# First phase of an encoder block: sine tables two steps later, gated weights in three parts, a third value buffer, and 20 instead of 25 weight conversions

## The reference

```python
h = rms_norm(x, norm1_gain)
proj = h @ w_in                      # (B, S, 1984)
g_q, g_k, g_v, g_gate, g_lr_f, g_lr_b, m_q_a, m_kv_a, m_k_rope = split(proj)
# A: gated linear attention, both directions, from g_q, g_k (256 columns each),
#    g_v (512), g_gate (512), g_lr (2 x 16)
# B: latent attention: mq = rms_norm(m_q_a) @ w_qb, mkv = rms_norm(m_kv_a) @ w_kvb,
#    norms per head, rotation of 32 of 96 columns by cos/sin(position * inv_freq), softmax
x = x + concat([gla_out, mla_out]) @ w_out
h = rms_norm(x, norm2_gain)
x = x + hierarchical_moe(h)          # 32 experts in 4 groups, top 1 group, top 2 experts
```

## Time and profile before

| What | Value |
|---|---|
| Median of 3 runs | 1159.68 us |
| Profiled execution | 1163.62 us |
| Span of core 7, first to last instruction | 1161.9 us |
| Spans of cores 0 to 3 | 1132.9, 1146.5, 1147.5, 1131.8 us |
| Spans of cores 4 to 7 | 1129.2, 1158.3, 1149.3, 1161.9 us |
| First reciprocal of cores 0 to 3 | 261.2, 279.0, 282.9, 261.2 us |
| First reciprocal of cores 4 to 7 | 259.7, 283.0, 266.3, 280.0 us |
| Busy over the span, core 7 | TensorE 69%, ScalarE 54%, VectorE 45%, GpSimd 41% |

### The profile page before, as it was taken

How to read it: one execution, slowest core, us unless ns; L and a number is a source line. 1 busy time by engine, 2 the same in 40 slices (tenths; PEclk the granted TensorE clock), 3 DMA queues, 4 the chain that set the end, 5 groups by cost and what they waited for, 6 DMA issues and landing times.

```text
span 1161.9 us, 18961 instructions; the slowest of 8 cores (1129.2 to 1161.9 us)
## 1 busy us (share of the span) xinstructions
PE 806.2 (69%) x5171; PEld 412.1 (35%) x5171; DVE 523.6 (45%) x857; ACT 627.4 (54%) x1008; POOL 471.3 (41%) x571
## 2 busy tenths in 40 slices
PE   0478778966787787888885786867612877655464
PEld 0244344432222222323221343433202765444452
DVE  3376547622666566666653335463650221221121
ACT  3568577736999999777773233333311543432231
POOL 3054446641555656434410211414243565444333
PEclk9789889988999999999998688777855998888887
DMA  8926976794878777888873587446786699999984
GB/s 145 176 90 116 128 166 127 124 154 99 122 119 132 113 116 101 127 106 118 134 153 81 101 166 197 94 143 152 203 212 216 166 243 244 246 257 262 264 204 75
DMA packets 87949, 179.86 MB, mean 155 GB/s; under 512 B 19129, under 2 KB 37339, under 8 KB 87780
## 3 DMA queue, kind: packets, MB, share of 16 engines
q0 software_dynamic: 36960, 82.53, 48.8%
q1 hardware_dynamic: 50580, 96.04, 27.7%
q10 hardware_dynamic: 304, 0.07, 0.0%
HBM read 201.75 MB, written 93.45 MB: 254 GB/s over the span
## 4 chain that ended last, share of the span: by engine, by line
PE 34%; ACT 15%; SPq 15%; issue 12%; DVE 12%; DMA 10%; POOL 1%; DVEq 1%; ACTq 1%; POOLq 0%
PE pb L444 32%; SPq L417 14%; ACT pbuf L421 7%; DVE rcb L1015 3%; DMA wsl<-w_bf 2%; PE pb L448 2%; DMA v_sp<-vst 2%; ACT sqj L421 2%; DMA xt<-x 2%; DVE PV L429 1%; DMA qk_sp<-qkst 1%; ACT L421 1%; DVE smb L429 1%; ACT sqn L421 1%; ACT rso L421 1%
## 5 line engine op out<-in xcount | busy, mean ns | idle before, releaser
L421 ACT ACTIVATE pbuf<-pb 128x1024 bf16<-128x1024 f32 x256 | 254.2, 1021 | 46.6 <-PE pb L444 43.9
L444 PE MATMUL pb<-pbuf,vA 128*128 128x512 bf16 x512 | 156.8, 382 | 55.3 <-ACT pbuf L421 53.3
L444 PE MATMUL pb<-qhT,khT 96*128 96x512 bf16 x512 | 155.0, 383 | 4.5 <-issue 4.5
L1015 DVE RECIPROCAL rcb<-pb 64x512 f32<-64x512 f32 x32 | 107.4, 3355 | 89.1 <-PE pb L444 88.9
L444 PE MATMUL pb<-xT,wsl 128*128 128x192 bf16 x1024 | 98.9, 262 | 45.8 <-DMA wsl<-w_bf 43.9
L444 PEld LDWEIGHTS pb<-xT,wsl 128*128 128x128 bf16 x1024 | 92.7, 104 | 49.8 <-issue 48.0
L1141 POOL DMA_INDIRECT out<-zb,LTm x32 | 50.9, 1592 | 117.7 <-ACT xT L421 53.1
L429 DVE TENSOR_TENSOR hid<-sil,pb 128x384 bf16<-128x384 f32 x32 | 17.7, 554 | 176.7 <-PE pb L444 166.0
L548 POOL DMA_DIRECT2D w_bf<-w_exp x112 | 58.5, 528 | 81.8 <-DVE mixM L429 39.1
L444 PEld LDWEIGHTS pb<-pbuf,vA 128*128 128x128 bf16 x512 | 35.4, 96 | 152.3 <-issue 144.8
L429 POOL TENSOR_TENSOR rg<-rg,gqkr 128x512 f32<-128x512 f32 (+1 forms) x32 | 32.1, 1002 | 120.0 <-DVE rg L429 117.7
(11 more groups left out here) (170 smaller groups left out, 1521.7 us busy)
## 6 DMA issues: line engine op xcount, KB each, us to landing
w_bf<-w_exp POOLq DMA_DIRECT2D x112, 384.0 KB, 7.3
wsl<-w_bf SPq DMA_DIRECT2D x112, 384.0 KB
xt<-x SPq DMA_DIRECT2D x32, 512.0 KB
out<-PV SPq DMA_DIRECT2D x16, 512.0 KB
wsl<-w_exp POOLq DMA_DIRECT2D x16, 384.0 KB
qk_sp<-qkst SPq DMA_DIRECT2D x16, 256.0 KB
PV<-qk_sp SPq DMA_DIRECT2D x16, 256.0 KB
h_tok<-hb SPq DMA_DIRECT2D x16, 256.0 KB
```

The source lines that it names most:

```text
L421: return op("act", lambda e: e.activation(out=out, in_=in_, func=func, **kw), reads=reads, writes=writes, n=fsz(out))
L444: return op("pe", lambda e: e.matmul(out, lhsT=lhsT, rhs=rhs, start=start, stop=stop), reads=reads, writes=writes, n=fsz(rhs) * (4 if rhs. ...
L1015: op("dve", lambda e, vrows=vrows, srows=srows, ob=ob: e.reciprocal(out=rcb[vrows, :], in_=P[ob][srows, :]), reads=[PN[ob]], writes=["rcb" ...
```

## The change

It touches the first phase and the table that spreads the conversions.

1. `rope_tables` becomes a generator. Its VectorE part stays where it was, with two tiles `yy0` and `yy1` in place of `yy`; its four ScalarE instructions move to the end of step 1.
2. `w_in_gla` is loaded as three loads of 512 columns with a name each (`wgqk`, `wgv`, `wgg`), the two `wlr` loads before the third, and 32 unused columns are not loaded. Each block waits only for its own part.
3. `vst` has a third tile.
4. `B2Q` interleaves the kinds: k, v, k / q, v, q / v, lr, v / four g.
5. `stage_small` runs in steps 4 to 6 rather than 5 to 7. Pieces: two in each of steps 7 to 16 (20 in all) rather than two or three in each of steps 8 to 17 (25). The attention rounds take three in six rounds of seven, 80 in all rather than 75.

```diff
--- before.py
+++ after.py
@@ -497,7 +497,7 @@
         wm = R("w_in_mla", [128, 8, 416], BF16)
         wqb = R("wqb", [128, 2, 768], BF16)
         wkvb = R("wkvb", [128, 1024], BF16)
-        wg = R("w_in_gla", [128, 8, 1568], BF16)
+        wg = R("w_in_gla", [128, 8, 1536], BF16)
         wlr = R("wlr", [128, 8, 64], BF16)
         cs = R("cs", [128, NT, 64], F32)
         gqa = R("gqa", [128, 384], F32)
@@ -521,7 +521,7 @@
         qkf = [R("qkf%d" % i, [128, 16, 96], BF16) for i in range(3)]
         MR = region(M0, QH0)
         qkst = [MR("qkst%d" % i, [128, 512], F32) for i in range(3)]
-        vst = [MR("vst%d" % i, [128, 512], BF16) for i in range(2)]
+        vst = [MR("vst%d" % i, [128, 512], BF16) for i in range(2)] + [R("vst2", [128, 512], BF16)]
         sgst = [MR("sgst%d" % i, [128, 512], BF16) for i in range(4)]
         lrst = MR("lrst", [64, 512], F32)
         waug = MR("waug", [64, 512], F32)
@@ -530,7 +530,7 @@
         kk = TR("kk", [128, NT, 16], F32)
         ki = TR("ki", [128, NT, 16], I32)
         rr = TR("rr", [128, NT, 16], F32)
-        yy = TR("yy", [128, NT, 16], F32)
+        yyL = [TR("yy%d" % i, [128, NT, 16], F32) for i in range(2)]
         m_ = TR("m_", [128, NT, 16], F32)
 
         ORDER = [g_ * 8 + j for j in range(8) for g_ in range(4)]
@@ -563,9 +563,11 @@
         dma("pool", wm[:, :, :], win_d.ap()[:, 1568:1984].rearrange("(c p) n -> p c n", p=128), writes=["wm"])
         dma("pool", wqb[:, :, :], wqb_d.ap().rearrange("(c p) n -> p c n", p=128), writes=["wqb"])
         dma("pool", wkvb[:, :], wkvb_d[:, :], writes=["wkvb"])
-        dma("pool", wg[:, :, :], win_d.ap()[:, 0:1568].rearrange("(c p) n -> p c n", p=128), writes=["wg"])
+        for nm_, c0_, c1_ in (("wgqk", 0, 512), ("wgv", 512, 1024)):
+            dma("pool", wg[:, :, c0_:c1_], win_d.ap()[:, c0_:c1_].rearrange("(c p) n -> p c n", p=128), writes=[nm_])
         dma("pool", wlr[:, :, 0:16], win_d.ap()[:, 1536:1552].rearrange("(c p) n -> p c n", p=128), reads=["wlr"], writes=["wlra"])
         dma("pool", wlr[:, :, 32:48], win_d.ap()[:, 1552:1568].rearrange("(c p) n -> p c n", p=128), reads=["wlr"], writes=["wlrb"])
+        dma("pool", wg[:, :, 1024:1536], win_d.ap()[:, 1024:1536].rearrange("(c p) n -> p c n", p=128), writes=["wgg"])
         dma("sp", gqa[:, 0:256], bcast_row(gqa_d, 256), writes=["gqaq"])
         dma("sp", gqa[:, 256:384], bcast_row(gkva_d, 128), writes=["gqak"])
         dma("sp", gqk[:, 0, :], bass.AP(gqn_d, 64, [[0, 128], [1, 32]]), writes=["gqkq"])
@@ -605,19 +607,19 @@
             stt(rr[:, :, :], kk[:, :, :], -C1, ang[:, :, :], ALU.mult, ALU.add, ["kk", "ang"], ["rr"])
             stt(rr[:, :, :], kk[:, :, :], -C2, rr[:, :, :], ALU.mult, ALU.add, ["kk", "rr"], ["rr"])
             for which, shift in ((1, 0.0), (0, PI / 2)):
...
-                if which == 0:
-                    act(cs[:, :, 0:16], yy[:, :, :], AF.Sin, ["yy"], ["cs"])
-                    act(cs[:, :, 16:32], yy[:, :, :], AF.Sin, ["yy"], ["cs"])
-                else:
-                    act(cs[:, :, 48:64], yy[:, :, :], AF.Sin, ["yy"], ["cs"])
-                    act(cs[:, :, 32:48], cs[:, :, 48:64], AF.Copy, ["cs"], ["cs"], scale=-1.0)
-            S.alias(["khT"], ["ang", "kk", "ki", "rr", "yy", "m_"])
+                yy, yn = yyL[which], "yy%d" % which
...
+            yield
+            act(cs[:, :, 0:16], yyL[0][:, :, :], AF.Sin, ["yy0"], ["cs"])
+            act(cs[:, :, 16:32], yyL[0][:, :, :], AF.Sin, ["yy0"], ["cs"])
+            act(cs[:, :, 48:64], yyL[1][:, :, :], AF.Sin, ["yy1"], ["cs"])
+            act(cs[:, :, 32:48], cs[:, :, 48:64], AF.Copy, ["cs"], ["cs"], scale=-1.0)
+            S.alias(["khT"], ["ang", "kk", "ki", "rr", "yy0", "yy1", "m_"])
 
         SQ2 = math.sqrt(2.0)
 
@@ -742,10 +744,10 @@
             if kind == "v":
                 t = 4 * g + idx
                 for kc in range(8):
-                    mm(P[bk][:, :], hT[:, kc, hslot(t)], wg[:, kc, 512:1024], kc == 0, kc == 7, [hname(t), "wg"], [PN[bk]])
-                st_ = vst[t % 2]
-                cp("dve", st_[:, :], P[bk][:, :], [PN[bk]], ["vst%d" % (t % 2)])
-                dma("sp", vsp[t * 128:(t + 1) * 128, :], st_[:, :], reads=["vst%d" % (t % 2)], writes=["vsp%d" % t])
+                    mm(P[bk][:, :], hT[:, kc, hslot(t)], wg[:, kc, 512:1024], kc == 0, kc == 7, [hname(t), "wgv"], [PN[bk]])
+                st_ = vst[t % 3]
+                cp("dve", st_[:, :], P[bk][:, :], [PN[bk]], ["vst%d" % (t % 3)])
+                dma("sp", vsp[t * 128:(t + 1) * 128, :], st_[:, :], reads=["vst%d" % (t % 3)], writes=["vsp%d" % t])
                 S.dma_since_barrier.pop()
                 return
             for kc in range(8):
@@ -758,7 +760,7 @@
                 else:
                     lhsT = wlr[:, kc, :]
                 mrows = 64 if kind == "lr" else 128
-                mm(P[bk][0:mrows, :], lhsT, hT[:, kc, gs], kc == 0, kc == 7, hn + ["wg", "wlra", "wlrb"], [PN[bk]])
+                mm(P[bk][0:mrows, :], lhsT, hT[:, kc, gs], kc == 0, kc == 7, hn + {"q": ["wgqk"], "k": ["wgqk"], "g": ["wgg"], "lr": ["wlra", "wlrb"]}[kind], [PN[bk]])
             if kind in ("q", "k"):
                 u = nst["qk"] % 3
                 nst["qk"] += 1
@@ -781,12 +783,13 @@
                 dma("sp", lrsp[g * 64:(g + 1) * 64, :], lrst[:, :], reads=["lrst"], writes=["lrsp%d" % g])
                 S.dma_since_barrier.pop()
 
-        B2Q = [[("k", 0), ("k", 1), ("q", 0)], [("q", 1), ("v", 0), ("v", 1)], [("v", 2), ("v", 3), ("lr", 0)],
+        B2Q = [[("k", 0), ("v", 0), ("k", 1)], [("q", 0), ("v", 1), ("q", 1)], [("v", 2), ("lr", 0), ("v", 3)],
                [("g", 0), ("g", 1), ("g", 2), ("g", 3)]]
         st_A1(0)
         late_consts()
         st_A1(1)
-        rope_tables()
+        rope = rope_tables()
+        next(rope)
         for step in range(NT + 5):
             def has(k):
                 return 0 <= step - k < NT
@@ -819,10 +822,12 @@
                 st_Lr(step - 2)
             while bq:
                 b2_block(*bq.pop(0))
-            if step in (5, 6, 7):
-                stage_small(step - 5)
-            elif 8 <= step <= 17:
-                for _ in range(2 + step % 2):
+            if step == 1:
+                next(rope, 0)
+            if step in (4, 5, 6):
+                stage_small(step - 4)
+            elif 7 <= step <= 16:
+                for _ in range(2):
                     stage_piece()
         S.barrier()
         PVf = A("PV", [128, NT, D], F32, at=W0)
@@ -1015,7 +1020,7 @@
                 op("dve", lambda e, vrows=vrows, srows=srows, ob=ob: e.reciprocal(out=rcb[vrows, :], in_=P[ob][srows, :]),
                    reads=[PN[ob]], writes=["rcb"], n=2500)
                 mo = tt("dve", mixM[vrows, h // 2, qsl], P[ob][vrows, :], rcb[vrows, :], ALU.mult, [PN[ob], "rcb"], ["mixM_%d" % (h // 2)])
-                for _ in range((3, 3, 2)[it % 3] if it < 28 else 0):
+                for _ in range((3, 3, 3, 3, 3, 3, 2)[it % 7] if it < 28 else 0):
                     stage_piece([mo])
                 if 1 <= it < 17:
                     d1_iter(it - 1)
```

More of the change, by code:

```diff
@@ L607, in rope_tables @@
             for which, shift in ((1, 0.0), (0, PI / 2)):
-                ts("dve", yy[:, :, :], rr[:, :, :], shift, None, ALU.add, None, ["rr"], ["yy"])
-                ts("dve", m_[:, :, :], yy[:, :, :], PI, None, ALU.is_gt, None, ["yy"], ["m_"])
-                stt(yy[:, :, :], m_[:, :, :], -2 * PI, yy[:, :, :], ALU.mult, ALU.add, ["m_", "yy"], ["yy"])
-                ts("dve", m_[:, :, :], yy[:, :, :], -PI, None, ALU.is_lt, None, ["yy"], ["m_"])
-                stt(yy[:, :, :], m_[:, :, :], 2 * PI, yy[:, :, :], ALU.mult, ALU.add, ["m_", "yy"], ["yy"])
-                ts("dve", yy[:, :, :], yy[:, :, :], PI, -PI, ALU.min, ALU.max, ["yy"], ["yy"])
-                if which == 0:
-                    act(cs[:, :, 0:16], yy[:, :, :], AF.Sin, ["yy"], ["cs"])
-                    act(cs[:, :, 16:32], yy[:, :, :], AF.Sin, ["yy"], ["cs"])
-                else:
-                    act(cs[:, :, 48:64], yy[:, :, :], AF.Sin, ["yy"], ["cs"])
-                    act(cs[:, :, 32:48], cs[:, :, 48:64], AF.Copy, ["cs"], ["cs"], scale=-1.0)
-            S.alias(["khT"], ["ang", "kk", "ki", "rr", "yy", "m_"])
+                yy, yn = yyL[which], "yy%d" % which
+                ts("dve", yy[:, :, :], rr[:, :, :], shift, None, ALU.add, None, ["rr"], [yn])
+                ts("dve", m_[:, :, :], yy[:, :, :], PI, None, ALU.is_gt, None, [yn], ["m_"])
+                stt(yy[:, :, :], m_[:, :, :], -2 * PI, yy[:, :, :], ALU.mult, ALU.add, ["m_", yn], [yn])
+                ts("dve", m_[:, :, :], yy[:, :, :], -PI, None, ALU.is_lt, None, [yn], ["m_"])
+                stt(yy[:, :, :], m_[:, :, :], 2 * PI, yy[:, :, :], ALU.mult, ALU.add, ["m_", yn], [yn])
+                ts("dve", yy[:, :, :], yy[:, :, :], PI, -PI, ALU.min, ALU.max, [yn], [yn])
+            yield
[4 more added lines that the diff above has]
```

(1 more changed line is left out.)

## The result

The changed kernel takes 1141.64 us (median of 4 runs, 1139.58 to 1147.39) against 1162.82 us for the kernel before in the same comparison (4 runs, 1157.51 to 1174.39). The ratio is 0.9864, with a 95% interval of 0.9821 to 0.9908. So it is faster by 1.4%, inside the border of 2%. The ratios compare executions in the faster of two states; of the traces, those of e1_stores, e4_sines and e10_six are from the slower one. The forecast was 1143 us. The profiled execution took 1142.63 us; its span is 1140.8 us, on core 5.

What follows compares the result with a forecast made beforehand. Bound: late cores' first phase, with VectorE waiting for stores. Core 7: 280.0 - 22.1 + 2.0 + 1.3 - 2.5 = 258.7, ending at 1140.6; core 6 slowest at 1143.0. Forecast 1143 us, range 1131 to 1156.

Steps and rivals of the forecast that it cites:

- the border of 2%: Whole kernel: 2% taken as what a measurement can tell from no change, so faster means under 1136.5 us.
- The stores: First phase, VectorE's copies: all waits for k and v stores go, 22.1 us on core 7, 6.1 on core 6.
- the residue: Steps 16 and 17: k or q copies still late, 2 us on core 7, 1 us on core 6, bounds 0 to 8.
- The rival in which the stall moves: Step 17's q copy or the third v copy stands instead, about half of 22.1 us left, 1151 us; chance 0.19.
- Fewer pieces: Five pieces move from first phase to attention at 0 us, at most 15; gain costed together with tile and order.
- The sines: Step 2 on ScalarE: a second table load on the chain costs +1.3 us, bounds 0 to +3.2.
- The load of the weights: Start: rows of 1024 bytes take about 141 ns, making the load +4.2 us over 16 engines, but hidden.
- Tile 3: Start: shorter weight rows shorten SyncE's queue turns, so x tile 3 lands 2.5 us earlier.
- Its outcome as the prediction worked it out: Start: queues switching only at packet boundaries leave tile 3 landing as before, start at +1.3 rather than -1.2 us.
- The sum: Whole kernel: first reciprocals at 258.7 and 260.0 us plus 881.9 and 883.0 on cores 7 and 6; core 6 last.
- the first rival: Whole phase faster by over 2%: core 6 has core 4's 869.5 us behind it, core 7 likewise, 1130 us; chance 0.16.
- The rival in which the cores meet: Behind the first phase: aligned cores read experts' weights at once, 8 to 12 us more, 1152 us; chance 0.09.

Runs made afterwards that it cites:

- e1_stores: Kernel before with the third value tile and the new block order only, weights in one load of 1536 columns; 1146.64 us, ratio 0.9951.
- e4_sines: Kernel before with only the sines moved to the end of step 1; 1162.38 us, ratio 0.9959.
- e10_six: Changed kernel with the gated weights in six loads of 256 columns, rows of 512 bytes; 1142.94 us, ratio 0.9872.
- e6: Changed kernel with the conversions as before: small copies in steps 5 to 7, 25 pieces in steps 8 to 17; 1140.63 us, ratio 0.9885.
- e2: Kernel before with only the conversions of the change: small ones a step earlier, 20 pieces, 80 in the attention; 1146.01 us, ratio 0.9906.
- the nine kernels taken together above: Five kernels with one weight load norm tile 3 at 36.2 us (mean of medians), four with three loads at 33.1 us.
- e3: Kernel before with only the gated weights in three loads; 1153.72 us, ratio 0.9998.
- e5: Changed kernel with two value tiles and the old block order; 1144.34 us, ratio 0.9915.

## Why the prediction was right, and where it was not

**The stores: right, the residue too high.** The 15.4 and 6.7 us of the earlier trace rows are 0 on all cores after. The sum took 22.1 off and put 2.0 back for core 7, a net of 20.1. Its stretch from the first `abT` copy to the first reciprocal went from 238.9 to 221.3 us, -17.6; without the +1.56 of the sines that is -19.2. So the net was right to 1 us by two errors: the q and k copies of steps 16 and 17 don't wait at all, and about 3 of the 22.1 us were slack. Slack shows on the cores with little to wait: core 4 had 6.8 us of waits in the kernel before, and its stretch was 221.7 us, 1.4 us over the 220.3 that it took in e1_stores. The rival in which the stall moves is out: half of it left over would have shown as waits on these lines.

**Fewer pieces: cost right, no gain once the tile and the order are in.** The prediction gave one answer for tile, order and pieces together. The experiments take them apart: e1 does all of it without the pieces, e6 loses nothing by putting them back. Alone, the conversions are in line with one step of the forecast, that the k store of step 8 lands in time once the fill of `row_list` is a step earlier (e2, no q or k copy waits); that the first group's v copies would then wait with two tiles was not foreseen. The moved pieces cost nothing in attention, as said: 343.4 us in the median over the cores, before 343.9, though from 300 to 440 us the conversions' queue of core 7 rose from the earlier trace rows to

```profile
q0 software_dynamic: 5024, 13.72, 87.4%
```

**The sines: right.** Forecast +1.3, measured +1.56 (e4). The window of 3.17 us hides the four sines and their table load only just, and a wait of 0.40 us inside them comes on top of the second load, which is on the path. The Trainium skill, page "ScalarE: Activation LUTs", section on what a table load costs, gives some 1283 ns for the load and 1380 ns of drain behind it. The rows agree on the load, 1.28 us; the 1.56 us by which step 2 grew for two more loads, one of them hidden, leave no room for a drain as long as that on the path. Behind either load the next activation starts within 0.01 us (37.81 and 42.25 us).

**The load of the weights: right on being hidden, wrong on its price.** The forecast had 141 ns for a row and +4.2 us for the load. A row takes 122 ns, and 3072 x 122 = 375 engine-us are no more than the 366 of the long rows. The first gated block runs at 63.18 us and waits for nothing.

```profile
63.18 2.05 PE L444 MATMUL pb<-hT,w_in_gla 128*128 128x512 bf16 x8
```

**Tile 3: direction and size near, the mechanism borne out in part.** The term was -2.5, from 14 turns of SyncE's queue. These two executions have 39.17 - 34.33 = 4.8 us on core 7 and 4.1 us in the median of the cores; over the nine kernels taken together above it is 3.1. The prediction's step was that the queues take turns row for row whatever the rows' size, so that a turn gets shorter with the row. Windows of 2 us test it in which both queues keep the 16 engines of core 7 full, or nearly so. While tile 3 itself is on its way, it holds on core 7. Before, 30 to 32 us, and after, 28 to 30 us:

```profile
q0 software_dynamic: 54, 0.17, 71.3%
q1 hardware_dynamic: 56, 0.17, 34.0%
```

```profile
q0 software_dynamic: 107, 0.12, 57.5%
q1 hardware_dynamic: 98, 0.20, 45.4%
```

It is one to one in both, and per row of SyncE's the load's queue takes 0.713 x 32 / 56 = 0.41 us before and 0.575 x 32 / 98 = 0.19 us after (32 is 16 engines times 2 us). On core 0 the window after has 200 to 71 rows already. A little later, with tile 4 on its way, it doesn't hold. Before, 38 to 40 us:

```profile
q0 software_dynamic: 65, 0.20, 60.8%
q1 hardware_dynamic: 67, 0.27, 38.1%
```

After, 36 to 38 us:

```profile
q0 software_dynamic: 179, 0.18, 68.5%
q1 hardware_dynamic: 64, 0.26, 39.7%
```

e10, 30 to 32 and 32 to 34 us:

```profile
q1 hardware_dynamic: 98, 0.37, 61.9%
q0 software_dynamic: 230, 0.12, 49.1%
```

```profile
q0 software_dynamic: 365, 0.19, 85.9%
q1 hardware_dynamic: 66, 0.24, 35.5%
```

With rows of 3136 bytes it is still one to one. With 1024 bytes it is 2.8 to one, and SyncE's queue has the same share as before, 39.7 against 38.1%, so nothing is gained there. With 512 bytes it is 2.3 and 5.5 to one in neighbouring windows. So the rows to a turn don't follow from their size alone, and what sets them is open. The Trainium skill, page "DMA: Bandwidth & Descriptors", section on queues, rings and completion order, has an engine switch queues only at packet boundaries. That several short rows go to a turn is in line with it, and its typical 9 to 17 descriptors is not, if a row is one: these windows show 1 to 5.5. Its outcome as the prediction worked it out, tile 3 landing as before, is not what e3 and e10 show either.

How much of the 3.1 us is shorter turns stays open. Another part may be a tail: before, from 34 to 36 us, with tile 3 still due on core 7, SyncE's queue has few rows, as if some engines alone were behind. After, from 32 to 34 us, it is close to its end already:

```profile
q0 software_dynamic: 90, 0.28, 97.4%
q1 hardware_dynamic: 23, 0.06, 12.1%
```

```profile
q0 software_dynamic: 258, 0.26, 102.4%
q1 hardware_dynamic: 18, 0.05, 10.4%
```

The trace doesn't say which engine a row went through, so this stays a hint.

**The sum: right on the first phase, wrong on which core is last.** Forecast and measured first reciprocal: core 7, 258.7 and 257.3 us; core 6, 260.0 and 256.6. The step that failed is that each core keeps what it took behind its first reciprocal, and that cores 6 and 7 are enough to look at. Core 7 did, 1138.2 - 257.3 = 880.9 against 881.9 us. Core 6 went from 883.0 to 1123.7 - 256.6 = 867.1, and core 5 from 875.3 to 882.1, and is now last at 1140.8. The sum never worked out core 5, which had stood longest for stores (27.1 us) and left the first phase last (283.0). Over the 11 traces without e1, e4 and e10 the stretch behind the first reciprocal has a median of 882.0 us on core 5, 880.9 on core 7 and 867.1 to 872.0 on the other six. The 883.0 us of core 6, on which the forecast stood, are 16 us above that core's median of 867.1. The total was near because some core has about 882 us behind it in both kernels; the sum didn't know which, and that it came out within 2 us is luck in this part. So core 6 did fall to what the first rival had assumed for it (869.5), but the kernel didn't, because that rival let core 7 keep pace with it. In the others of these 11 the longest stretch lies between 872.1 (e2) and 892.6 us (e5). This is most of the scatter of whole times, and none of the experiments aimed at it.

**The rival in which the cores meet: open.** Its 8 to 12 us more behind the first phase didn't come: the median over the cores is 875.1 us, before 871.2. Core 5 and its neighbour, core 4, show no rule: core 5's stretch is 882.1 us after, where it leaves the first phase 5.8 us behind core 4, 892.6 in e5, 7.8 us ahead of it, 869.7 in e1, 2.9 us behind, and 875.3 in the kernel before, 23.3 us behind. Over the 88 cores of the 11 traces the stretch is shorter where the mean granted clock is higher (correlation -0.6) and hardly goes with how far apart cores 0 and 1, 2 and 3, 4 and 5, 6 and 7 leave the first phase (-0.1). Neither is a cause shown, and no run here settles it.

## What to carry to other kernels

When an engine in written order stands for its own stores, give the staging tile one more buffer and put blocks of other kinds between its uses: the buffer alone left waits here, both together none (the order alone was not run), and the traffic beside the stores could stay as it was. Sum up per core, since a stall that differs from core to core is worth only what the slowest core gets back, and don't take what one core needed behind it in one execution as lasting. An activation that needs another table costs its second load wherever ScalarE is the chain, so put it where the engine waits anyway, and so that the load back falls into a wait too.

## What had not been expected of the hardware

- Rows of a casting load cost in proportion to their bytes down to 512: 357, 122 and 56 ns for 3136, 1024 and 512 bytes written. A fixed part per row doesn't show between these three; but early in the kernel, at 10 to 20 us, rows of 846 bytes on average took 123 ns.
- Two queues that keep the engines full share them row for row while the load's rows are long (54 to 56 and 65 to 67 rows with 3136 bytes). With shorter rows the share varies: 107 to 98 and 179 to 64 with about 1024 bytes, 230 to 98 and 365 to 66 with 512.
- A store's landing doesn't go with its size alone: 15.69 us for a k store and 12.78 us for a v store of half its bytes. With the small conversions a step earlier and five pieces fewer, the waits for stores fell from 16.6 to 5.0 us in the median over the cores (e2).
- Copies of one program leave the first phase 23 us apart before and 7 us apart after. What remains is the arrival of x tiles 2 and 3 (30.3 to 37.0 us for the norm of tile 3); behind it the cores agree within 1.7 us.
